# A fused two-block transformer kernel on one core: four of twelve modulation units are reduced by GpSimd during layer 1's input projections instead of by TensorE during its attention

## The reference, cut to what matters

```
mod   = silu(c)     @ w_mod + b_mod          # w_mod is 1024 x 6144
mod_c = silu(c_ctx) @ w_mod + b_mod
sh1, sc1, gt1, sh2, sc2, gt2 = split(mod, 6)
csh1, csc1, ...              = split(mod_c, 6)   # only the first two of mod_c are used
```

## Time and profile before

| what | value |
|---|---|
| time, median of 3 runs | 1182.54 us (1180.65 to 1185.15) |
| the profiled execution, its own time | 1182.84 us |
| its span in the trace | 1180.9 us |
| PE busy | 1013.8 us (86%) |
| DVE busy | 428.1 us (36%) |
| ACT busy | 237.0 us (20%) |
| POOL busy | 54.4 us (5%), 70 instructions |
| granted TensorE clock, mean | 0.951 |
| bytes moved by DMA | 323.68 MB, 274 GB/s over the span |

### The profile page before, as it was taken

One profiled execution on the slowest core, in us unless ns is written; L12 is line 12 of the kernel. 1 busy time (PEld: TensorE's weight loads), 2 busy tenths in 40 slices (PEclk: granted clock), 3 DMA queues, 4 the chain that ended last, 5 costly groups with the idle time before them and its releaser, 6 DMA issues.

```text
span 1180.9 us, 18175 instructions
## 1 busy us (share of the span) xinstructions
PE 1013.8 (86%) x7714; PEld 528.9 (45%) x7714; DVE 428.1 (36%) x1021; ACT 237.0 (20%) x587; POOL 54.4 (5%) x70
## 2 busy tenths in 40 slices
PE   5999999999999999998998898988666766766666
PEld 2344764444576457885577765432111111111112
DVE  1137755433863646354257764311000000000002
ACT  0012144111313514624122332110000000000002
POOL 0101000000100000001113300000000000000000
PEclk9999999999999999999998998998888888888789
DMA  9973357443347964013210347999999999999996
GB/s 384 414 289 143 117 219 307 144 168 135 143 177 291 429 243 161 12 60 143 99 49 3 123 174 281 399 426 429 431 428 429 430 430 429 430 431 427 433 429 275
DMA packets 28159, 323.68 MB, mean 274 GB/s; under 512 B 3264, under 2 KB 3392, under 8 KB 5808
## 3 DMA queue, kind: packets, MB, share of 16 engines
q1 hardware_dynamic: 26048, 314.18, 64.7%
q0 software_dynamic: 2032, 8.35, 2.0%
HBM read 321.47 MB, written 1.05 MB: 273 GB/s over the span
## 4 chain that ended last, share of the span: by engine, by line
PE 62%; DMA 31%; DVE 3%; issue 2%; ACT 1%; SPq 1%; DVEq 0%; ACTq 0%
PE banks L657 50%; DMA scr_qk<-in_stream 14%; DMA ring<-in_stream 8%; DMA Vt_to_O<-in_stream 6%; DMA zuv_to_Kt<-in_stream 3%; PE banks L668 3%; PE banks L2221 1%; PE banks L929 1%; PE banks L807 1%; PE banks L950 1%; PE banks L915 1%; PE banks L912 1%; SPq L563 1%; PE banks L920 0%; PE banks L953 0%
## 5 line engine op out<-in xcount | busy, mean ns | idle before, releaser
L657 PE MATMUL banks<-ring,uT 128*128 128x512 f32 (+1 forms) x512 | 223.0, 589 | 3.6 <-issue 2.3
L657 PEld LDWEIGHTS banks<-ring,uT 128*128 128x128 f32 x512 | 95.1, 190 | 115.8 <-issue 113.1
L657 PE MATMUL banks<-ring,scr_qk 128*32 128x512 f32 (+1 forms) x496 | 82.5, 619 | 28.6 <-DMA ring<-in_stream 28.1
L657 PE MATMUL banks<-scr_qk 64*64 64x64 f32 (+2 forms) x2368 | 84.1, 266 | 24.0 <-DMA scr_qk<-in_stream 19.4
L2787 DVE SCALAR_TENSOR_TENSOR UWK<-UWK,banks 128x256 f32<-128x256 f32 x16 | 6.7, 421 | 268.1 <-ACT UWK L3069 268.1
L657 PE MATMUL banks<-ring,UWK 128*32 128x512 f32 (+1 forms) x336 | 85.0, 781 | 11.7 <-ACT UWK L3077 8.1
L3069 ACT ACTIVATE UWK<-banks 128x256 f32<-128x256 f32 x16 | 6.1, 383 | 361.6 <-PE banks L657 361.6
L657 PEld LDWEIGHTS banks<-scr_qk 64*64 64x64 f32 (+2 forms) x2368 | 55.9, 135 | 47.9 <-issue 36.0
L657 PE MATMUL banks<-UWK,ring 128*128 128x256 f32 x320 | 71.0, 380 | 0.0
L2221 PE MATMUL banks<-UWK 128*128 128x512 f32 x128 | 66.4, 643 | 0.9 <-DVE UWK L2795 0.9
L657 PEld LDWEIGHTS banks<-UWK,ring 128*128 128x128 f32 x320 | 60.4, 190 | 9.3 <-issue 1.4
(11 more groups left out here) (385 smaller groups left out, 1228.3 us busy)
## 6 DMA issues: line engine op xcount, KB each, us to landing
ring<-in_stream SPq DMA_DIRECT2D x93, 2048.0 KB, 17.3
scr_qk<-in_stream SPq DMA_DIRECT2D x11, 2048.0 KB, 39.5
Vt_to_O<-in_stream SPq DMA_DIRECT2D x11, 2048.0 KB, 38.9
zuv_to_Kt<-in_stream SPq DMA_DIRECT2D x10, 2048.0 KB, 39.4
scr_qk<-in_stream SPq DMA_DIRECT2D x11, 1024.0 KB, 41.3
wide<-in_stream SPq DMA_DIRECT2D x10, 1024.0 KB, 38.2
const<-in_stream SPq DMA_DIRECT2D x10, 1024.0 KB, 37.1
misc<-in_stream SPq DMA_DIRECT2D x10, 1024.0 KB, 39.3
```

The lines of the kernel that those rows point to most:

```text
L657: return pe.matmul(o, a, b, start=start, stop=stop)
```

## The change

Units 4 to 7 of `w_mod` are streamed earlier: 4 and 5 behind projection group 1 of layer 1, 6 and 7 behind group 3. PE passes over them in its list of units. GpSimd multiplies each in place by the vector (4096 values in each partition), adds the eight blocks of 512 in three halvings (2048, 1024, 512 values), and writes the sum over blocks to a part of `gT`, which is free at that time. Units 4, 5 and 6 are done ahead of the fox rows, unit 7 behind them. Ahead of the gate columns PE adds the 128 partitions of the four parts with one matmul each (`pe_mod_parts`), with a column of ones as the window, into the same rows of bank 7; units 0 to 3 and 8 to 11 are added on top as before. In the attention, PE multiplies units 8 to 11 in the steps m = 2, 4, 6, 8. `v_mod_window` moves to layer 0, ahead of its attention.

```diff
+SIDE = (4, 5, 6, 7)
+ONE_AT = 2 * SIDE[-1]
...
-            if l + 1 == DEPTH and cg == 6:
-                for c in range(2):
+            if l + 1 == DEPTH and cg in (1, 3, 6):
+                for c in {1: SIDE[0:2], 3: SIDE[2:4], 6: (0, 1)}[cg]:
                     cols("w_mod_2", 0, c * 512, 512, "mod_mm", c)
...
-            for cg in range(2, 12):
+            for cg in (2, 3) + tuple(range(8, 12)):
                 cols("w_mod_2", 0, cg * 512, 512, "mod_mm", cg)
...
+            while units[unit_at[0]] in side:
+                unit_at[0] += 1
             k = unit_at[0]
...
+            pool.memset(onewin, 0.0).then_inc(*tick("pool_step"))
+            pool.wait_ge(*last("pool_step"))
+            pool.memset(onewin[:, ONE_AT:ONE_AT + 1], 1.0).then_inc(*tick("pool_step", "onewin"))
...
+        def pool_mod_part(pool, j):
+            u = units.index(("mod_mm", SIDE[j]))
+            w = held(slot[u]).rearrange("p (k n) -> p k n", n=512)
+            pool.wait_ge(K.sem(f"arrived{slot[u]}"), 16 * use[u])
+            c = modwin[:, :, MOD_AT:MOD_AT + 1].broadcast_to([P, DCH, 512])
+            pool.tensor_tensor(w, w, c, ALU.mult).then_inc(*tick("pool_step"))
+            for n in (4, 2):
+                pool.wait_ge(*last("pool_step"))
+                pool.tensor_tensor(w[:, 0:n, :], w[:, 0:n, :], w[:, n:2 * n, :], ALU.add).then_inc(*tick("pool_step"))
+            pool.wait_ge(*last("pool_step"))
+            pool.tensor_tensor(part(j), w[:, 0, :], w[:, 1, :], ALU.add).then_inc(*tick("pool_step", "mod_mm", SIDE[j]))
...
+            if l + 1 == DEPTH:
+                pool.wait_ge(*at("mod_mm", "window"))
+                for k in range(DCH):
+                    pool.wait_ge(*at("mixT", l - 1, k))
+                for j in range(3):
+                    pool_mod_part(pool, j)
             pool.wait_ge(*at("h", l, 3, 0))
             pool.wait_ge(*at("h", l, 3, 1))
...
             if l == DEPTH - 1:
+                pool_mod_part(pool, 3)
                 pool.wait_ge(*at("scores", l, 0, 1))
...
-            pe_rows(pe, ("mod_mm",), modwin, MOD_AT, 2, n, 0, 11, 7)
+            pe_rows(pe, ("mod_mm",), modwin, MOD_AT, 2, n, "parts", 11, 7)
...
+        def pe_mod_parts(pe):
+
+            pe.wait_ge(*free(7))
+            pe.wait_ge(*at("onewin"))
+            for j, n in enumerate(SIDE):
+                pe.wait_ge(*at("mod_mm", n))
+                lo = ONE_AT - 2 * n
+                ins = pe.matmul(bank[7][32 * j:32 * j + 32, :], onewin[:, lo:lo + 32], part(j), start=True, stop=False)
+            ins.then_inc(*fill(7, "mod_mm", "parts"))
...
-                    elif m < 10:
-                        pe_mod_rows(pe, 2 + m)
+                    elif m < 10 and m % 2 == 0:
+                        pe_mod_rows(pe, 7 + m // 2)
...
             w = take(pe)
+            if l + 1 == DEPTH:
+                pe_mod_parts(pe)
             pe_gate_cols(pe, l, 0, w)
...
                 v_rows(dve, l, 1)
-                v_mod_window(dve)
...
                 v_window(dve, l + 1)
+                v_mod_window(dve)
             v_attend(dve, l)
```

More of the change, by code:

```diff
@@ L350, in build @@
         modwin = sb("modwin", DCH, MOD_AT + 32, stack=one)[:, :, :]
+        onewin = sb("onewin", ONE_AT + 32 - 2 * SIDE[0], stack=one)[:, :]
         w1 = sb("w1", 2, LPAIR, HD, stack=one)
@@ L508, in build @@
         unit_at = [0]
+        side = [("mod_mm", n) for n in SIDE]
         def take(pe, n=512):
+            while units[unit_at[0]] in side:
+                unit_at[0] += 1
             k = unit_at[0]
@@ L684, in pe_mod_rows, with part @@
         def pe_mod_rows(pe, n):
-            pe_rows(pe, ("mod_mm",), modwin, MOD_AT, 2, n, 0, 11, 7)
+            pe_rows(pe, ("mod_mm",), modwin, MOD_AT, 2, n, "parts", 11, 7)
+        def part(j):
+            return gT[:, 2 * j:2 * j + 2, :].rearrange("p a s -> p (a s)")
+        def pe_mod_parts(pe):
[6 more added lines that the diff above has]
+            ins.then_inc(*fill(7, "mod_mm", "parts"))
         def pe_ada_columns(pe, l, half=0):
```

## The result

The changed kernel takes **1201.39 us** (median of 4 runs, 1196.63 to 1203.80) against 1183.51 us of the kernel before in the same comparison (4 runs, 1180.65 to 1185.15): ratio **1.0147**, 95% interval 1.0115 to 1.0179, so 17.9 us slower. The profiled execution took 1203.80 us with a span of 1202.0 us and a mean granted clock of 0.937 (before: 1182.84, 1180.9 and 0.951).

The account below looks back on a forecast made before the run. Layer 1 was taken as bound by PE's own work. Terms -7.4 + 1.4 - 0.5 + 0.9 + 1.0 + 3.3 + 14.0 = +12.7 us on 1182.84 gave 1195.5 us (1190 to 1201; whole range 1178 to 1208).

Parts of the forecast that it names:

- the lost race: Rival, layer 1 projections: unit 6's multiply stops the rope's last instructions, +5 to +11 us, say 1204 us; chance 0.15.
- The product's length: GpSimd's work in layer 1: 7.0 us for the multiply of 4096 values, 15.1 us a unit.
- I take it to be stopped too: DVE's scaling ending layer 0's normalisation waits for unit 4's multiply, delaying PE's transposes: +3.3 us.
- The load of projection 2: Layer 1: projection 2's weights go into projection 0's slot and land after PE ends projection 1: +1.0 us.
- The index sums: Layer 1: unit 7 stops DVE's two-operand index sums, so PE waits at the cumulative sum, then transposes: +14.0 us.
- The attention: Layer 1: four units leave PE (-7.4), steps without one wait for softmax (+1.4), late-unit waits go (-0.5 us).
- The parts: Layer 1: PE's four added matmuls side by side are half a unit's eight: +0.9 us.
- DVE reads PSUM only: Layer 1, 15 us after the rope: unit 6 on GpSimd stops no DVE instruction: 0 us.
- Giving way: Rival: GpSimd lets DVE in within an instruction, each DVE wait about 0.9 us; +4.4 us, 1187 us; chance 0.12.
- Side by side: Rival: GpSimd's products and DVE's work hardly meet, leaving loads and extra matmuls; -4.6 us, 1178 us; chance 0.18.

Follow-up runs that it names:

- experiment 4: Changed kernel with GpSimd starting unit 4 only after the scaling of layer 0's residual rows; 1210.84 us, ratio 1.0230.
- experiment 8: Changed kernel with only units 4 and 5 on GpSimd, behind the scaling and the rope, units 6 to 11 on PE; 1182.73 us, ratio 1.0001.
- experiment 3: Changed kernel with only units 4, 5 and 6 on GpSimd, unit 7 back in PE's attention; 1185.91 us, ratio 1.0011.
- experiment 5: Changed kernel with all four units on GpSimd, unit 7 held until the index sums have ended; 1184.96 us, ratio 1.0017.
- experiment 2: Changed kernel with GpSimd's products and sums cut into instructions of 512 values, 15 a unit instead of 4; 1197.04 us, ratio 1.0116.
- experiment 1: Changed kernel with GpSimd's products and sums replaced by memsets about as long that read no SBUF; 1177.44 us, ratio 0.9962.
- experiment 6: Changed kernel with four units on GpSimd, units 4, 6 and 7 held behind the scaling, the rope and the index sums; 1184.34 us, ratio 1.0009.
- experiment 7: Changed kernel with units 4 to 6 on GpSimd, unit 7 on PE, units 4 and 6 held behind the scaling and the rope; 1184.04 us, ratio 1.0009.

## Why the prediction was right, point by point

The direction, the mechanism and the range held; the time was 5.9 us above the forecast (1201.4 against 1195.5), 0.4 us above the forecast's own range and inside the whole one. The time alone would have pointed to the wrong rival: it lies in the 1200 to 1206 us of the lost race. The trace decides, since the rope was over before unit 6 came. Without the clock the measured terms of layer 1 make 17.4 + 1.0 - 5.9 = 12.5 us, against the 12.7 of the sum.

- **The product's length** was 7.0 us for the multiply and 15.1 us a unit; measured 7.03, 6.93 for the two larger adds together, 1.26: 15.2 us. Taking each slope from its like was right.
- **"I take it to be stopped too"** (the scaling, +3.3 us): 3.2 us of wait. Experiments 4 and 8, with unit 4 behind it, have the scaling back at its length and no wait for it.
- **The load of projection 2** (+1.0 us): 0.99 us.
- **The index sums** (+14.0 us): 13.2 us, in one wait ahead of the cumulative sum, where the prediction had split it into some 12 and 2. DVE got in as written, one instruction behind each of GpSimd's. Experiments 3 and 5 take the wait away and with it 15.5 and 16.4 us.
- **The attention** (-7.4 + 1.4 - 0.5 = -6.5 us): -5.9 us. **The parts** (+0.9): 1.0 us.
- **The term that is missing: the clock behind the waits.** The sum of the prediction had each stop at the length of the wait and PE at full clock after it. Rows of this stage before could not show it, since PE waited nowhere in it for more than 0.9 us; after, the windows behind both waits stand at 0.50, and 6.0 us are lost. With it the prediction's 12.7 us become 18.7, against 17.9 over the runs. The Trainium skill (TensorE: Matmul & The Clock Gate, The HAM clock gate) says that an idle array is clocked at 1.2 GHz and a busy one at 2.4; the windows at 0.50 agree, and the prediction had not weighed it against its own two waits.
- **The rope's race** was the first rival, with a margin of about 1 us. The margin was 4.1 us. In experiment 5, where no low clock followed the first wait, it was 1.9 us (279.40 to 281.28), so the low clock made some 2 us of it. Unit 6's load also took 13.4 us (273.82 to 287.24), not 11.6. Experiment 4 shows the lost race and its price: 15.6 us of waits, above the rival's +5 to +11 us. Against the change the first wait of 3.2 us went, and the low clock behind the rope's waits (about 3.4 us) made up for the low clock that went with it; layer 1 of the profiled run is 12.4 us longer than in the change. The medians differ by 9.5 us. Behind layer 1 the profiled run of experiment 4 is 2.6 us shorter than that of the change, and why is not shown.
- **"DVE reads PSUM only"** beside unit 6 was not quite so: the two gate products read SBUF as well. They were not stopped, and the **0** held.
- **Giving way** (rival 2) falls by the 7329 ns index sum and experiment 2. **Side by side** (rival 3) falls by experiment 1, which also agrees with its sum: 1178 us by the prediction, 1177.4 measured when GpSimd reads nothing. The row that spoke for this rival, index sums that keep their length beside POOL's L640, is the GpSimd TENSOR_SCALAR shown under experiment 1, which does not stop them after the change either.

The rule that the prediction weighed (the Trainium skill, SBUF — State Buffer, Who interferes with whom) is borne out in both its halves beside products and memsets: two-operand instructions are kept out where GpSimd reads (7329 ns) and not where it only writes (at most 480 ns). Beside GpSimd's TENSOR_SCALAR it is not: there two index sums took 0.50 and 0.47 us, and the measurement decides.

## What to carry to other kernels

An idle GpSimd is not a free engine: before giving it an elementwise product, list the DVE instructions in that stretch that read two SBUF operands (and ones like the scaling and the rope's copy here, which were stopped with one), and count up to one GpSimd instruction's length for each. A stop that reaches PE can cost more than the wait, since the clock behind it may be low, and a stop that is removed can move a load into the next one: after each repair the race behind it has to be worked out anew. The gain was 0.4% at best, so a single stop of 7 us decided it.

## What the runs showed of the hardware that was not expected

- A GpSimd memset, which reads nothing, stretched DVE's TENSOR_SCALAR of 1024 values from 0.81 to 2.54 us, and the index sums not at all (at most 480 ns). The same section of the Trainium skill (SBUF — State Buffer, Who interferes with whom) names TENSOR_SCALAR and copies among the instructions that can contend with GpSimd. The scaling (6.09 us beside a product) and experiment 4's copy of 0.23 us that lasted 6.94 agree; no run shows a copy beside a memset alone.
- After the 3.2 us wait PE ran at the low clock in the change and in experiment 3 (transposes 1.97 us in both), but not in experiment 5 (1.09 us); after the 13.2 us wait it did in both traces that have it. Behind the wait for the rope it did in experiment 6 (2.0 us of waiting, then four matmuls in 3.08 us instead of 1.95) and not in experiment 7 (2.2 us, then 1.88). So a wait of 2 to 3 us may or may not bring the low clock.
- GpSimd loses too: the adds of unit 5 took 7.79 and 2.12 us beside DVE's row products, where undisturbed ones take 6.93 and 1.26.
